# Two gates of a recurrence in one step: four 64x64 products on the quarters of TensorE's array, with exchanged halves put back by ScalarE

## The reference, cut to what matters

```
xb = xc.reshape(B, T, N_RG_BLOCKS, RG_BLOCK)              # 8 blocks of 64 channels
r = sigmoid(einsum('btnd,nde->btne', xb, wa) + ba)        # recurrence gate
i = sigmoid(einsum('btnd,nde->btne', xb, wx) + bx)        # input gate
log_a = -RG_C * r * softplus(-lam)
a = exp(log_a)
u = sqrt(maximum(1 - exp(2 * log_a), 0)) * (i * xc)
h_t = a_t * h_{t-1} + u_t                                  # scanned forward, and backward
```

## Time and profile before

| what | value |
|---|---|
| median of 3 runs | 1010.83 us (1008.39 to 1011.78) |
| profiled execution | 1011.6 us, span 1009.8 us |
| TensorE busy | 880.2 us, 87% of the span |
| VectorE, ScalarE busy | 342.5 us, 249.5 us |
| chain that ended last | PE 49%, DMA 35%, SyncE's queue 5%, DVE 4%, ACT 2% |
| HBM read | 287.16 MB, 313 GB/s over the span with the writes |

### The profile page before, as it was taken

The page is one execution under the profiler, slowest core; times in us unless marked ns, Lnnn a source line. Parts: engine busy times, 40 slices in busy tenths (PEclk is TensorE's granted clock), DMA queues, the critical chain, the costliest instruction groups (busy, mean ns, idle before and its releaser), DMA issues.

```text
span 1009.8 us, 12030 instructions
## 1 busy us (share of the span) xinstructions
PE 880.2 (87%) x4242; PEld 509.2 (50%) x4242; DVE 342.5 (34%) x845; ACT 249.5 (25%) x418; POOL 157.0 (16%) x210
## 2 busy tenths in 40 slices
PE   4799898999999999999896887978878989978974
PEld 2388776899898954443332333423333334333421
DVE  1653553577574553233221212111211111212115
ACT  2546613443333321121211101111111111111111
POOL 7200000000001320222121121211212212212111
PEclk9799989999999999999998988988989989989988
DMA  9974868322237397899999999999999999999914
GB/s 343 348 254 151 291 209 236 98 84 84 84 125 283 142 377 291 299 355 387 396 388 407 374 382 388 370 375 384 351 369 389 357 375 389 357 375 388 370 46 187
DMA packets 90123, 299.44 MB, mean 297 GB/s; under 512 B 18182, under 2 KB 40770, under 8 KB 65121
## 3 DMA queue, kind: packets, MB, share of 16 engines
q1 hardware_dynamic: 67472, 263.21, 66.4%
q0 software_dynamic: 13904, 31.13, 11.4%
q10 hardware_dynamic: 8704, 4.54, 1.8%
HBM read 287.16 MB, written 29.10 MB: 313 GB/s over the span
## 4 chain that ended last, share of the span: by engine, by line
PE 49%; DMA 35%; SPq 5%; DVE 4%; ACT 2%; issue 2%; POOL 1%; ACTq 1%; POOLq 0%; DVEq 0%
DMA gu<-in_w_up_e_dram 32%; PE bank L1407 14%; PE bank L1038 7%; PE bank L1040 6%; PE bank L1039 6%; PE bank L1426 3%; SPq L477 3%; PE bank L1066 2%; PE bank L1300 2%; DMA y_dram<-y_sb,slot_row 2%; PE bank L1107 1%; DMA chunk_raw<-in_w_ada_dram 1%; SPq L488 1%; PE bank L1395 1%; PE bank L1133 1%
## 5 line engine op out<-in xcount | busy, mean ns | idle before, releaser
L1407 PE MATMUL bank<-gu,x_t 128*64 128x512 f32 (+1 forms) x1024 | 312.5, 657 | 74.4 <-DMA gu<-in_w_up_e_dram 72.9
L1407 PEld LDWEIGHTS bank<-gu,x_t 128*64 128x64 f32 (+1 forms) x1024 | 110.8, 164 | 244.5 <-issue 210.2
L1426 PE MATMUL bank<-dn,a_t 128*64 128x512 f32 (+1 forms) x512 | 145.3, 597 | 4.8 <-ACT shared_sb L973 3.5
L712 POOL DMA_INDIRECT y_dram<-y_sb,slot_row x39 | 62.7, 1607 | 467.0 <-issue 243.4
L1888 DVE TENSOR_TENSOR act_sb<-silu_sb,bank 128x256 f32<-128x256 f32 x40 | 16.9, 421 | 327.4 <-ACT silu_sb L1008 327.4
L1008 ACT ACTIVATE silu_sb<-bank 128x256 f32<-128x256 f32 x40 | 15.4, 385 | 347.6 <-PE bank L1407 347.6
L1426 PEld LDWEIGHTS bank<-dn,a_t 128*64 128x64 f32 (+1 forms) x512 | 48.5, 150 | 74.8 <-issue 67.5
L1038 PE MATMUL bank<-h_hi,chunk_lo 128*128 128x384 f32 x240 | 85.1, 355 | 0.0
L999 ACT ACTIVATE y_sb<-bank,slot_gate 128x512 f32<-128x512 f32 x80 | 50.6, 684 | 126.1 <-PE bank L1426 106.4
L1040 PE MATMUL bank<-h_hi,chunk_hi 128*128 128x384 f32 x240 | 81.4, 339 | 0.0
L1039 PE MATMUL bank<-h_lo,chunk_hi 128*128 128x384 f32 x240 | 81.3, 339 | 0.0
(11 more groups left out here) (336 smaller groups left out, 1027.0 us busy)
## 6 DMA issues: line engine op xcount, KB each, us to landing
gu<-in_w_gate_e_dram SPq DMA_DIRECT2D x64, 1024.0 KB, 17.1
gu<-in_w_up_e_dram SPq DMA_DIRECT2D x64, 1024.0 KB, 27.2
dn<-in_w_down_e_dram SPq DMA_DIRECT2D x64, 1024.0 KB, 26.2
chunk_raw<-in_w_ada_dram SPq DMA_DIRECT2D x24, 1024.0 KB, 8.7
chunk_raw<-in_w_in_dram SPq DMA_DIRECT2D x18, 1024.0 KB, 5.4
chunk_raw<-in_w_out_dram SPq DMA_DIRECT2D x4, 1024.0 KB, 4.9
y_dram<-zeros POOLq DMA_DIRECT2D x1, 3072.0 KB, 18.2
chunk_raw<-in_w_pa_dram SPq DMA_DIRECT2D x2, 1024.0 KB, 5.0
```

The source lines that it names most:

```text
L712: pool.indirect_dma_start(y_dram[:, :], bass.IndirectOffsetOnAxis(ap=slot_row[:, u % UN:u % UN + 1], axis=0), y_sb[u % 2][:, :], None, bou ...
L1407: mm = pe.matmul(bank[2 + u % 2][at_x, :].rearrange("p (g n) -> p g n", g=2), x_t[:, cols], wide[:, :, k, :], start=(k == 0), stop=(k == K ...
L1426: mm = pe.matmul(bank[5 + half][at_x, :], a_t[:, cols], dn[slot_of(x, first)][:, wc], start=(k == 0), stop=(k == 1))
```

## The change

The loop over 16 products becomes a loop over 8 pairs (d, t). For each, four 64x64 products are issued: for gate r the two blocks in place, for gate i the two blocks with the output halves exchanged, so that each of the four works in another quarter of the array (`par` chooses the rows, `par ^ kind` the output half). Gate r goes to bank 0 or 4, gate i to bank 1 or 5. One semaphore increment follows the four. Group n waits for the activations of group n-2.

ScalarE now runs three activations for each group: one of 128 partitions for gate r, and two of 64 partitions for gate i, each from the other half of the bank. It increments `gates_tanh` behind the first and behind the third, so that 16 is still the last value.

```diff
-            for n in range(16):
-                kind, d, t = n // 8, n // CT % 2, n % CT
+            for n in range(8):
+                d, t = n // CT, n % CT
                 act.wait_ge(S["gates_mm"], n + 1)
-                j = kind * 8 + d * CT + t
-                act.activation((gate_r, gate_i)[kind][:, d, t, :], bank[(0, 1, 4, 5)[n % 4]][:, 0:RC], ACT.Tanh, scale=0.5,
-                               bias=half_b[:, j:j + 1]).then_inc(S["gates_tanh"], 1)
+                act.activation(gate_r[:, d, t, :], bank[(0, 4)[n % 2]][:, 0:RC], ACT.Tanh, scale=0.5,
+                               bias=half_b[:, n:n + 1]).then_inc(S["gates_tanh"], 1)
+                for par in range(2):
+                    ins = act.activation(gate_i[half_rows(par), d, t, :], bank[(0, 4)[n % 2] + 1][half_rows(1 - par), 0:RC], ACT.Tanh,
+                                         scale=0.5, bias=half_b[half_rows(par), 8 + n:9 + n])
+                ins.then_inc(S["gates_tanh"], 1)
             act.wait_ge(S["gates_tanh"], 16)
...
-            for n in range(16):
-                kind, d, t = n // 8, n // CT % 2, n % CT
-                if n >= 4:
-                    pe.wait_ge(S["gates_tanh"], n - 3)
-                pe.matmul(bank[(0, 1, 4, 5)[n % 4]][:, 0:RC], block_w[:, d, kind, t, :], xc[:, t, :],
-                          start=True, stop=True).then_inc(S["gates_mm"], 1)
+
+            for n in range(8):
+                d, t = n // CT, n % CT
+                if n >= 2:
+                    pe.wait_ge(S["gates_tanh"], 2 * n - 2)
+                for kind in range(2):
+                    for par in range(2):
+                        mm = pe.matmul(bank[(0, 4)[n % 2] + kind][half_rows(par ^ kind), 0:RC],
+                                       block_w[half_rows(par), d, kind, t, DH * par:DH * par + DH], xc[half_rows(par), t, :],
+                                       start=True, stop=True)
+                mm.then_inc(S["gates_mm"], 1)
```

## The result

| kernel | median us | lowest, highest | runs |
|---|---|---|---|
| before | 1010.68 | 1007.19, 1013.65 | 11 |
| changed | 1019.68 | 1013.15, 1022.32 | 11 |

The ratio is 1.0078, interval [1.0053, 1.0103]: slower, with an interval clear of 1, and outside my range of 1010.8 to 1017.0. The eleven times of the changed kernel fall into two groups: 1013.15, 1013.73, 1015.03 and 1015.62, then seven from 1019.67 to 1022.32. The means of the groups are 1014.4 and 1021.0. The mean granted clock of each run goes with them: 0.942 to 0.949 in the four, 0.933 to 0.939 in the seven. The profiled execution is the shortest, 1013.15 us (span 1011.4). It therefore shows the cost of the gates, but not what separates the two groups.

What follows compares the result with a forecast made beforehand. TensorE was taken to bound the gates before, ScalarE after. A later TensorE (1.13 us) plus a clock fall (1.5) gave +2.6 us on the profiled 1011.6, 1014.2, so a median of 1013.4 us; range 1010.8 to 1017.0.

Steps and rivals of the forecast that it cites:

- The path and the bound: Gates stage: on the path, bound by TensorE before the change and by ScalarE after it, 1.41 against 0.65 us a group.
- a later TensorE at 80 us moves the end: Behind the gates: the experts' loads start when TensorE releases them, so its delay moves the end by the same amount.
- A group costs 3 x 0.47 = 1.41 us: ScalarE in the gates: three activations for each group, starting 0.47 us apart, half partitions saving nothing.
- The clock in the gates: TensorE's pause of some 2.4 us after two groups lowers its clock to 1.2 GHz; taken as +1.5 us.
- 1.13: End of the gates: ScalarE's pace starts the projection at 80.93 instead of 79.80, TensorE 1.13 us later.
- TensorE runs on without a pause: Behind the gates: TensorE continues without pausing, so its delay passes on to the experts' loads; no size of its own.
- the halves in one bank don't run together: Rival, gate products: row halves sharing a bank run in turn, 1.3 us a group, +3.4 us, 1014.2 us; chance 0.12.
- Half the partitions at half the time: Rival, ScalarE in the gates: 64-partition activations cost half the time, -1.7 us, 1009.1 us; chance 0.04.
- The long low clock: Rival, gates into the projections: the clock falls and stays low, say +4.6 us, 1015.4 us; chance 0.17.
- The covers: Behind the gates: 2.1 us delay hidden in idle time, ScalarE's 3.65 us before its evacuation, VectorE's 6.09 before the row copy.

Runs made afterwards that it cites:

- delay4_route: Kernel before with six idle products (3.9 us) behind the gates and two in TensorE's pause ahead of the routing: 1014.96 us, ratio 1.0054.
- after_route: Changed kernel with two idle 512-column products in TensorE's pause ahead of the routing: 1014.60 us, ratio 1.0047.
- warm: Changed kernel with idle products in the gates, four before group 2 and one before each later group: 1015.25 us, ratio 1.0064.
- delay4: Kernel before, gates untouched, with six idle products (3.9 us) behind the gates: 1021.29 us, ratio 1.0116.
- swapped: Changed kernel, but VectorE copies the input with halves exchanged, 16 activations of 128 partitions, Tanh table loaded early: 1011.29 us, ratio 1.0011 against the kernel before.
- before_all: Kernel before with idle products in three pauses (122, 173, 345 us) and the Tanh table loaded ahead of the gates: 1009.54 us, ratio 0.9992.
- swapped_all: `swapped` plus the idle products of before_all in the three pauses: 1005.66 us, ratio 0.9961 against the kernel before.

## Why the prediction was wrong

**The path and the bound.** Right: ScalarE became the bound of the stage, and a later TensorE at 80 us moves the end. The second part is shown by delay4_route: 3.9 us put in behind the gates came out as 5.3, and after_route's +4.8 stands to 4.1 in the stage.

**"A group costs 3 x 0.47 = 1.41 us": this term was mis-sized.** It is 1.81. The last group started 79.49 - 66.34 = 13.15 us into the stage, where I had 80.11 + 0.06 - 69.24 = 10.93: 2.2 us, which is 17 x (0.60 - 0.47). The durations that I took were right: the 64-partition activations last 0.58 us like the full ones. I read from the earlier trace rows that half the partitions save nothing, and then gave them the 0.47 us step of the earlier trace rows, which full activations of the same partitions had shown. A step between starts is the duration less an overlap of 0.11 us, and no row showed that overlap for a change of partitions. The Trainium skill ("ScalarE: Activation LUTs", "What ACT_TABLE_LOAD costs") gives it without a condition: back-to-back activations overlap by about 93 ns. The trace nearly agrees for full ones (0.58 - 0.47 = 0.11) and not for these (0.60 apart).

**The clock in the gates.** The mechanism was right: a pause of 2.59 us, then a fall. The price was 0.7 us in the last group (1.50 us from its start to the projection, 0.76 at full clock in my sum; `warm` gives the same 0.7) and some 0.2 us for 0.4 us of projection at the low clock, together 0.9 where I took 1.5. The rest was hidden, because ScalarE's true period left room for a group at 1.2 GHz. The stage, up to the projection's start: 1.13 + 2.2 + 0.7 = 4.0, measured +4.1.

**The term that was missing.** "TensorE runs on without a pause" behind the stage was wrong; there are pauses that I didn't price, and the shift changed what one of them costs. I priced the clock only where the instructions change. In the pause ahead of the routing the profiled execution of the kernel before stays at full clock. Of the changed kernel's two, one stays and one falls, and by their times most of its runs fall. A fall costs about 6 us: 6.3 between delay4 and delay4_route, 1021.0 - 1014.4 = 6.6 between the two groups of the changed kernel, 5.1 to 5.4 between the changed kernel's medians and after_route. This was the larger part of the miss in the median. Sum: 4.1 in the gates and 6.3 in a fall make +10.4 in a run that has one, 1021.1 us; without one 1014.8. The two groups of runs stand at 1021.0 and 1014.4.

**The rivals.** That the halves in one bank don't run together is refuted: two groups in 1.53 us, 16 records. By the rule of the Trainium skill ("TensorEngine Tiling (Array Packing)", "Gotcha 1: PSUM Pressure") they would have needed about twice that, as they did on two quarters only (2.82 us); the measurement decides here, for this shape. Half the partitions at half the time is refuted too (0.58 us). The long low clock came close in its number, 1015.4 against 1014.4 for the short runs, but by luck: only 0.4 us of projection was slow. The covers held: ScalarE still idled 2.63 us before its evacuation (3.65) and VectorE 5.08 us before the row copy (6.09).

**What stays open.** Why the same pause, with the same work in it, falls in one execution and holds in another. That a shift alone makes long runs the rule is shown by delay4, and that idle products in the pause take them away by delay4_route; that the kernel before has long runs too, 5 of 35 above 1013 us in one set and 9 of 100 over all, fits. Which shifts are good and which bad isn't shown. The time of the pause doesn't settle it: the 48 products behind it start at 348.41 in the kernel before (full clock) and at 348.65 in `swapped` (low for a short stretch), at 351.52 in one execution of the changed kernel (full) and at 352.00 in the other (low). Open is also why before_all gained nothing, and where swapped_all got 2.4 of its 4.0 us.

## What to carry to other kernels

When you divide a step so that one engine gains, take the pace of the other engine from rows of the very shape and partitions that it will have; a start-to-start pace and a duration are two numbers, and the difference may depend on the neighbour. A shift of a few microseconds can cost more than itself (here 11.6 us for 3.9): list every pause of TensorE behind the change, ask which of them stands near a fall of the clock, and hold the clock there with idle products before you judge a small change. If halves must be exchanged, exchange them on an engine that has time (here eight small copies of the input on VectorE, which made the stage 1.6 us shorter than before the change, though the total fell only with idle products added), not on the one that sets the pace.

## What the hardware showed that I had not expected

- Four 64x64 float32 products on the four quarters of the array take about 0.7 us for 387 columns (two groups in 1.53 with the last one's end), also where two row halves write to one bank. On two quarters the same four take about 1.3 us (2.82 for two groups).
- Activations of 387 columns that wait for nothing start 0.47 us apart where all cover the same 128 partitions, and 0.60 apart where 128 partitions and exchanged halves of 64 alternate, at the same duration of 0.58 us.
- 3.9 us of idle products some 270 us ahead of a pause cost 11.6 us; two idle products of 512 columns in that pause give 6.3 of them back.
- The gates start at 66.3 to 69.4 us in the fourteen profiled executions, later the longer the clock was low between 28 and 44 us. One profile against one other can hide or feign 3 us.
